# A kernel of 29,360 instructions ordered by a planner: its costs for products, stores and loads, and two transfers as items apart from the copies behind them

## The reference

```python
# first block
h = rmsnorm(x, norm_w); proj = h @ w_in          # 4 x 512 (attention) + 4 x 512 (delta rule) + 16 gate columns
aq, ak = rmsnorm per head of 64; attn = neighbourhood_attention(aq, ak, av, rpb) * silu(az)   # 8 heads, 8 x 16 window on a 16 x 64 grid
qkv = silu(depthwise_conv5(concat(dq, dk, dv))); dq, dk = l2norm per head of 128
o = gated_delta(dq, dk, dv, forward gates) + flipped gated_delta(backward gates)              # 4 heads, a triangular solve and a recursion over chunks
delta = rmsnorm(o) * dn_norm_w * silu(dz)
x1 = x + concat(attn, delta) @ w_out
# second block
proj = rms_norm(x1) @ w_in2                       # 10 x 1024 columns
out_a = stick_breaking_attention(8 heads of 128) * silu(sb_g)
out_b = rms_norm(chunkwise_retention(4 heads of 256)) * silu(r_g)
merged = sigmoid(m_sb) * (out_a @ w_branch_sb) + sigmoid(m_ret) * (out_b @ w_branch_ret)
out = x1 + merged @ w_out2
```

## Time and profile before

| | us |
|---|---|
| median of 3 runs (2366.27 to 2379.09) | 2374.32 |
| the profiled execution, its own time | 2361.78 |
| its span, first to last instruction | 2360.0 |
| PE (TensorE) busy | 2235.7 |
| PE weight loads busy | 1822.7 |
| DVE busy | 1073.0 |
| ACT busy | 954.2 |
| POOL busy | 369.5 |

### The profile page before, as it was taken

How to read it: one execution, slowest core, us unless ns; L and a number is a source line. 1 busy time by engine, 2 the same in 40 slices (tenths; PEclk the granted TensorE clock), 3 DMA queues, 4 the chain that set the end, 5 groups by cost and what they waited for, 6 DMA issues and landing times.

```text
span 2360.0 us, 29360 instructions
## 1 busy us (share of the span) xinstructions
PE 2235.7 (95%) x11727; PEld 1822.7 (77%) x11727; DVE 1073.0 (45%) x1986; ACT 954.2 (40%) x1729; POOL 369.5 (16%) x610
## 2 busy tenths in 40 slices
PE   7999988998997899999999999999999999999998
PEld 6788776766786788778888877777888888788776
DVE  4344444353356343556556555644623434424431
ACT  4464543342554143446455555643232323223210
POOL 3100112364413020000000000003300212010011
PEclk9999988998898899999999999999999999999999
DMA  5521335455453331111111211012221112343222
GB/s 159 198 77 60 85 121 148 117 134 164 154 188 90 118 125 48 37 50 59 44 51 41 72 45 45 29 33 69 81 67 44 51 49 85 107 146 123 81 94 85
DMA packets 169961, 210.82 MB, mean 89 GB/s; under 512 B 36368, under 2 KB 122848, under 8 KB 168288
## 3 DMA queue, kind: packets, MB, share of 16 engines
q1 hardware_dynamic: 148848, 140.71, 19.4%
q0 software_dynamic: 20976, 68.23, 8.9%
HBM read 151.45 MB, written 53.77 MB: 87 GB/s over the span
## 4 chain that ended last, share of the span: by engine, by line
PE 82%; DVE 7%; ACT 5%; DMA 3%; issue 2%; POOL 1%; SPq 1%; DVEq 0%; POOLq 0%; ACTq 0%
PE PS L1551 18%; PE PS L1553 18%; PE PS L1552 18%; PE PS L1519 6%; PE PS L1825 3%; PE PS L1804 2%; PE PS L1545 2%; PE PS L1546 2%; PE PS L1547 2%; PE PS L1615 2%; PE PS L1634 2%; DVE WH L2243 1%; PE PS L1861 1%; PE PS L1874 1%; DMA RAW<-in_w_in 1%
## 5 line engine op out<-in xcount | busy, mean ns | idle before, releaser
L1551 PE MATMUL PS<-WH,HH 128*128 128x512 f32 x2112 | 867.2, 411 | 18.6 <-DVE WH L2243 8.3
L1553 PE MATMUL PS<-WH,HL 128*128 128x512 f32 x2112 | 831.6, 394 | 0.0
L1552 PE MATMUL PS<-WH,HH 128*128 128x512 f32 x2112 | 829.4, 393 | 0.0
L1551 PEld LDWEIGHTS PS<-WH,HH 128*128 128x128 f32 x2112 | 401.1, 190 | 106.3 <-DVE WH L2243 10.6
L1553 PEld LDWEIGHTS PS<-WH,HL 128*128 128x128 f32 x2112 | 400.0, 189 | 87.2
L1552 PEld LDWEIGHTS PS<-WH,HH 128*128 128x128 f32 x2112 | 401.7, 190 | 72.4
L2243 DVE SCALAR_TENSOR_TENSOR WH<-RAW,WK,WH 128x512 fp32r<-128x512 f32 (+2 forms) x248 | 181.7, 753 | 240.4 <-ACT WH L1883 239.5
L1883 ACT ACTIVATE TM<-PS 128x512 f32<-128x512 f32 (+3 forms) x285 | 154.7, 556 | 321.8 <-PE PS L1553 250.6
L1883 ACT ACTIVATE WH<-RAW,WK 128x512 fp32r<-128x512 f32 (+2 forms) x248 | 170.2, 705 | 83.5 <-DMA RAW<-in_w_in 41.7
L1519 PE MATMUL PS<-WK,TM 128*128 128x128 f32 x776 | 121.4, 286 | 48.7 <-DVE TM L2316 15.3
L1519 PEld LDWEIGHTS PS<-WK,TM 128*128 128x128 f32 x776 | 97.1, 147 | 75.2 <-DVE TM L2316 16.8
(11 more groups left out here) (306 smaller groups left out, 2783.6 us busy)
## 6 DMA issues: line engine op xcount, KB each, us to landing
RAW<-in_w_in SPq DMA_DIRECT2D x200, 256.0 KB, 2.9
RAW<-in_w_out SPq DMA_DIRECT2D x32, 256.0 KB, 3.5
sig_d<-WK POOLq DMA_DIRECT2D x32, 256.0 KB, 2.5
WK<-sig_d POOLq DMA_DIRECT2D x32, 256.0 KB, 3.5
WK<-in_rpb POOLq DMA_DIRECT2D x16, 480.0 KB, 4.8
RAW<-in_w_in SPq DMA_DIRECT2D x32, 192.0 KB, 3.4
dnc_d<-TM SPq DMA_DIRECT2D x12, 512.0 KB, 3.4
TM<-dnc_d SPq DMA_DIRECT2D x10, 512.0 KB, 4.8
```

The costliest lines, as they stand in the source:

```text
L1551: e.matmul(ps, hh, wt[:, 0:width], start=k == 0, stop=False)
L1552: e.matmul(ps, hh, wt[:, 512:512 + width], start=False, stop=False)
L1553: mm = e.matmul(ps, hl, wt[:, 0:width], start=False, stop=k == 7)
```

## The change

Items that cost nothing in the plan before, or too little, get other costs: `g` 685 ns for 660, `ns` 2.2 n for 1.75 n (n is 288 or 384 columns), `no` 810 for 680, `cw` 4800 for nothing, `pk` 4500 for 3500, `pg` 6200 for 4500, `pa` 4000 for 3000. `aside` puts an item without moving its chain's time, and `after` moves that time to where the item is done: the store `cw` runs beside square and norm, and `co` comes when both are done. `d8` becomes `d7` (the eight transfers on SP, 10000 ns) and, after a `yield`, `d8` (ACT's copies and GpSimd's ones). The ring that head 3's recursion leaves keeps what banks under 6 it had, and `free_banks` adds to the ring where it replaced an empty one. No instruction is added or removed.

```diff
+    def aside(self, *item):
+        begin = self.now[0]
+        self.put(*item)
+        self.now[0] = begin
+
+    def after(self, *item):
+        self.now[0] = max(self.now[0], self.known[item])
...
-        return {"ns": [("pe", 1.75 * n), dve(n + 90), act(n + 340)], "np": [("pe", 340), act(384)],
-                "no": [("pe", 680), ("dve", 440)]}[kind]
+        return {"ns": [("pe", 2.2 * n), dve(n + 90), act(n + 340)], "np": [("pe", 340), act(384)],
+                "no": [("pe", 810), ("dve", 440)]}[kind]
...
-        "g": [("pe", 660)],
+        "g": [("pe", 685)],
...
-        "pk": [("dma", 3500)],
-        "pg": [("dma", 4500)],
+        "cw": [("dma", 4800)],
+        "pk": [("dma", 4500)],
+        "pg": [("dma", 6200)],
         "pl": [("dma", 3000)],
-        "pa": [("dma", 3000)],
+        "pa": [("dma", 4000)],
...
-        "d8": [("dma", 8000), act(1024), ("pool", 200)],
+        "d7": [("dma", 10000)],
+        "d8": [act(1024), ("pool", 200)],
...
-        put("cw", h, c)
+        plan.aside("cw", h, c)
...
             put("d3", h)
+        plan.after("cw", h, c)
         put("co", h, c)
...
+            put("d7", n)
+            yield
             put("d8", n)
...
-            use_ring([], "rec3")
+            use_ring([b for b in state["ring"] if b < 6], "rec3")
...
-        if not state["ring"]:
-            use_ring([0, 1, 4, 5])
+        if 0 not in state["ring"]:
+            use_ring([0, 1, 4, 5] + state["ring"])
...
-                elif kind == "d8":
+                elif kind == "d7":
```

## The result

The changed kernel takes 2381.74 us (median of 10 runs, 2368.72 to 2385.76), the kernel before, beside it, 2367.36 (10 runs, 2361.53 to 2379.09): ratio 1.006, 95% interval 1.004 to 1.008. It is 0.6% slower where 0.6% faster was forecast. The profiled execution took 2385.14 us (span 2383.3, mean clock 0.956) against 2361.78 (span 2360.0, 0.965) before: +23.4 us, where the medians are 14.4 apart.

The account below looks back on a forecast made before the run. TensorE was taken as the bound, busy 95% of the span, with 124 us idle plus low-clock time to win. Terms summed to -14.6 us: 2347.2 from the profiled run, 2360 us on the median, range 2332 to 2388.

Parts of the forecast that it names:

- -4.5: Gate rows: PE's wait on a square sum behind DVE's first stand goes, -4.5 us, range 0 to -4.5.
- -1.7: Clock in the slice where that square-sum wait ends: half of 3.4 us lost at most, -1.7 us.
- -1.5: SP's queue at 368 us: weight loads no longer stand behind pg, -1.5 us, between 0 and -2.2.
- -1.8: Split of d8, n = 0: PE's wait before ACT's copy of lt_d goes, -1.8 us.
- -2.5: Split of d8, n = 0: half of the 4.9 us lost to the low clock after PE's wait, -2.5 us.
- 2.6: Split of d8, n = 1: ACT's last evictions, and the chain PE idles on, start earlier, -2.6 us.
- Product costs: New g, ns, no costs: better order removes small PE waits after 780 us, -3 us, bounds -16 to +16.
- The cost on the other side: Planned solve chain lengthens 30 us, products 27, so d9(1) comes 3 us later: +3 us, 0 to +15.
- late heads: Rival: more d9(1) parts fall behind POOL's table load, heads 2 and 3 start late; 13 us, 2387 us, chance 0.15.
- The clock: Clock lost after PE's waits before 570 us: half of 3.4 and 4.9 us taken, -1.7 and -2.5 us.

Follow-up runs that it names:

- e3: The changed kernel with the loads for heads 0 and 1 held until d7 of heads 2 and 3; 2342.02 us, ratio 0.9896 to the kernel before.
- e9: The changed kernel with a further, overwritten 128-partition matmul before each ns of the last attention pair; ratio 1.0077 to the kernel before.
- e10: e3 with a further, overwritten 128-partition matmul before each ns of the last attention pair; ratio 0.989 to the kernel before.
- e2: The kernel before with only the new cw, pk, pg, pa costs, aside, after and ring rules; median 2370.06 us, ratio 1.0011.
- e5: The kernel before with only d8 split into d7 and d8, plus the new ring rules; ratio 1.0042 to the kernel before.
- e7: e2 with the loads for heads 0 and 1 held until d8 of heads 2 and 3; ratio 0.9977 to the kernel before.
- e8: e3 with the lt_d store put beside the chain of solve by aside; ratio 0.9897 to the kernel before.
- e6: The kernel before with only g at 685 ns, plus the new ring rules; ratio 1.0096 to the kernel before.

## Why the prediction was wrong

**The stage that the change corrects: right, and too small.** -4.5, -1.7, -1.5, -1.8 and -2.5 are -12.0 us; the first stage moved by -15.0 in after, and by -21.7 to -24.9 in e3, e9 and e10, which have the same list up to there; DVE's 13.3 us of stands went to 2.3. The wait before the last pair went from 7.79 to 4.89 us, 2.9 for a forecast of 2.6. The single terms weren't additive, though: the split alone made ACT's second stand longer, and g alone cost 1%. So the runs bear out the way and the rough size of the sum, and not each term.

**Product costs: perhaps right, by the wrong reason.** For the order after the attention I took -3 us; that part came out 6.9 shorter in the profile of after. It isn't idle time, as I had it (39.8 us before, 39.4 after). The four profiles with the old `g` (before, e2, e5, e7) have 1581.2 to 1584.2 us there, the nine with the new one 1574.2 to 1581.0. That speaks for a gain of some microseconds, though e8 with 1581.0 is as long as before; it is busy time, and what makes it shorter isn't shown. What `g` does alone, in the first stage, I had not costed: +10.6 us in e6.

**"The cost on the other side": the step that failed.** I took the chain of `solve` to move 30 us in the plan and the products 27, a difference of 3, and priced it at +3. In the list that the changed program makes, the last `pa` is planned 40 us later and the last product 15 us later: the attention's new costs, 13.5 of my 27 us, hardly delay that product. The pass moves from 16 products ahead of the last one to behind it. That alone would have been the rival of late heads. What neither the sum nor the rival held is the release there: `share`, the chain that puts the image loads, releases those of heads 0 and 1 at the last product, and a store that comes behind it stands in SP's queue behind 14 loads. The store-to-transfer distance went from 3.1 to 21.2 us, `d7` moved by 32.4 us, d9's end by 51.3 and the stretch by 45.2, against the +3 less 2.6 that I had for it. I also asked of POOL only how many parts fall behind the table load, and never whether some fall behind `nw`: two did, and stood 29.1 us there.

**The rival came nearer.** "Late heads", 2387 us at 0.15, named place and effect: parts of d9(1) behind the table load (13 and not 12 of 15), heads 2 and 3 late, clock lost. Its 2387 us lie near the 2381.74 measured, but that is in part luck: its price was 13 us and the stretch's 45, offset by what the first stage gained. It was that rival's mechanism in POOL's queue, with a trigger that it didn't have, the loads ahead of the store. And parts behind the table load don't cost by themselves: e3 has all fifteen there. I had read SP's queue only at 368 us; the same view at 553 us, with the question of which items `share` puts there, would have shown the release of 14 loads 12 us behind the store.

**The clock.** I counted half of what the 10-us windows allowed. The loss in after is mostly of this kind: of the 45.2 us, 31.5 are busy time, at a clock of 0.73 for 0.82. The Trainium skill, TensorE: Matmul & The Clock Gate, section "Why this matters for your kernels", puts a lost rate down to idle gaps between bursts of matmuls. The two falls of the trace fit that, in waits of 4.9 and 6.7 us; the 50 us at 0.50 from 610 to 660, with PE busy for 9.8 to 10 us of each 10, are not explained by it.

## What to carry to other kernels

When planned costs are corrected, find every place where an item is released by a due time or by another item's end, and see on which side of it the moved items now fall: here a shift of the planned times did its harm by crossing such a point. Corrections of single costs don't add up: here `g` alone cost 1%, the product costs alone 2%, the load costs alone nothing, and all together 0.6%. So measure the parts and the whole. And where an in-order queue carries both bulk loads and a store that a chain waits for, try to hold the loads until the chain's transfers are issued: here this one line was worth 1.6% and made the change a gain of 1%.

## What the runs showed of the hardware

The same kernel, with the same order of instructions, varies by 30 us with its granted clock: e5 took 2360.66 us at a mean clock of 0.970 and 2392.01 at 0.954, the kernel before from 2352.3 (0.969) to 2386.07 (0.953). The six runs of e3 span under 5 us. Single stages differ too: up to the last attention product the lists of after, e3, e9 and e10 are the same, and they took 223.2 us (clock 0.94), 216.5, 215.9 and 213.3 (0.98 each). By these four, a difference below some 10 us in one stage is not to be read from one profile each.

An at_d store whose issue took 0.55 us in before and in e3 took 5.96 us behind the 14 loads, and the twelfth of these loads 7.68. The same store landed 21.1 us after its issue, with the DMA engines' share at 1.03, where the transfers that wait for it followed after 3.1 us in before.
